# The squares for an RMS norm added up to one tile on VectorE, so that TensorE sums one product in place of two

## The chip, the cores and the metric

One core of one Trainium2 chip. The metric is the device time of one execution of the whole program in microseconds (us), as the median of several runs.

## The reference

The program runs two layers of a hybrid mixer (mLSTM, gated linear attention, sparse attention), and then one block of another kind: a feed-forward part, a mixer (attention and spatial gating), and a second feed-forward part with a final norm. The batch is 1, the sequence 256 tokens, the width 1024, all in float32. In front of each part stands the same norm:

```python
def rmsnorm(x, g):
    xf = x.astype(jnp.float32)
    y = xf * lax.rsqrt(jnp.mean(xf * xf, axis=-1, keepdims=True) + EPS)
    return (y * g.astype(jnp.float32)).astype(x.dtype)

h = h + 0.5 * swiglu(rmsnorm_2(h, ffn1_norm[l]), ffn1_w_gate[l], ffn1_w_up[l], ffn1_w_down[l])
n = rmsnorm_2(h, mix_norm[l])
z = n @ w_in[l]                      # and the mixer on z, which ends with h = h + merged @ w_out[l]
h = h + 0.5 * swiglu(rmsnorm_2(h, ffn2_norm[l]), ffn2_w_gate[l], ffn2_w_up[l], ffn2_w_down[l])
```

What matters here is the mean over the 1024 channels of the squares of each token.

## The kernel before

The residual `x` lies as 8 tiles of 128 channels by 256 tokens. Weights stream in slots of 512 KB (a slot is a 128x1024 tile): SyncE loads a slot into `raw`, ScalarE copies it to the high part in `ring` (L481), and GpSimd (L367, in two pieces of 128x512) or, for some slots, VectorE (L1011, in one piece of 128x1024) subtracts to get the low part. TensorE multiplies high and low parts in three products for each pair of tiles; `slots_used` is its signal that a slot may be filled again.

The norm is not waited for. TensorE starts each part with products on `x` times the gain (`early`, L498, and `early_lo`, L1021), and the factor 1/root(mean) is multiplied into the results afterwards. The parts are numbered: n = 0 and 1 are the two layers, n = 2 the first feed-forward part, n = 3 the mixer, n = 4 the second feed-forward part. For each of them:

- ScalarE squares `x` in four blocks of 128x512 (`squares`, L487); block 0 goes to PSUM, into `ps[3]`.
- VectorE adds the other three to it (`add_squares`, L1028). The first two of these adds stay in PSUM, the third writes its 512 columns to `sqs`, a view of the tile `y`, and releases `sq_sum`. Each add but the last is followed by a wait for its own end (`step`).
- TensorE sums over the partitions: after the first two slots and half of the third (`around_squares`, L1746), it multiplies `ones` with the two halves of `sqs[:, 0:512]`, in `ps[4]` (`sum_squares`, L1726). The wait on `sq_sum` stands in front of the weight load of the first of these products. It then goes on with the other half of the third slot and with the fourth.
- VectorE makes the mean of it (L1004), ScalarE the logarithm and the exponential (L468, L469), VectorE one step of refinement (L1040 to L1044); the factor is then in `rms`. On ScalarE copies of weights (L481) stand between in program order.
- In a feed-forward part VectorE then makes the gate and the up product of tile 0 from the waiting results (L1478, L1483), and L1488, L1492 and L1073 go on with them; TensorE needs the bank of gate 0 for tile 2, after the fourth slot. In the mixer VectorE scales four early results (L1629) and TensorE needs the first of their banks after the fourth slot too.

At n = 4 one more instruction of VectorE stands between its adds and the mean: `split(FFN2_AT - 1)`, the low part of one slot (L1011). At n = 2 and n = 3 none does. The end of the program sums its last squares in another way (L1691, L2350), which the change does not touch.

Of the kernel before, what the change touches and what calls it, by code (L numbers as in the profile page):

```python
# [24 lines left out]
ALU = mybir.AluOpType  # L25
# [5 lines left out]
T = 256  # L31
KT = D // P
LAYERS = 2
# [101 lines left out]
GELU_A, GELU_B = 0.044715, 0.7978845608028654  # L135
N_UPDATES = 4
FINAL = LAYERS + 3
FINAL_AT = (LAYERS + 1) * (KT // 2)


# [14 lines left out]
def build(nc, d, out):  # L155
    ctx = ExitStack()
    with ctx:
# [54 lines left out]
        sqs = y[:, 8:16, :].rearrange("p a t -> p (a t)")  # L212
# [17 lines left out]
        def branch(k, part):  # L230

            return ys[:, k, part, :] if k < 4 else xs[:, k - 4, part, :]
# [18 lines left out]
        ps = [ctx.enter_context(nc.psum_tensor(f"ps{b}", [P, 512], F32)) for b in range(8)]  # L251
# [15 lines left out]
        ones = const[:, C_ONE:C_ONE + P]  # L267
# [23 lines left out]
        def _(sp):  # L291
# [55 lines left out]
            for k in (0, 2, 6, 4):  # L347
                if k == 6:
                    sp.wait_ge(S["last_f"], 1)
                else:  # L350
                    sp.wait_ge(S["x_f"], FINAL_AT + k // 2 + 1)
                sp.dma_start(out[:, k:k + 2, :], xn[:, k:k + 2, :]).then_inc(S["stored"], 16)
# [637 lines left out]
        def _(dve):  # L990
            step = Steps(dve, S["dve_steps"])
            tt, ts, stt = dve.tensor_tensor, dve.tensor_scalar, dve.scalar_tensor_tensor
# [10 lines left out]
            def mean_square(dst, src, n, done):  # L1003
                ts(dst, src, 1.0 / n, EPS, ALU.mult, ALU.add).then_inc(done, 1)  # L1004
# [19 lines left out]
            def add_squares(n):  # L1024

                for b in range(1, 4):
                    dve.wait_ge(S["sq"], n * 4 + b + 1)
                    ins = tt(ps[3][:, :] if b < 3 else sqs[:, 0:512], ps[3][:, :], sqs[:, b * 512:(b + 1) * 512],  # L1028
                             ALU.add)
                    if b < 3:  # L1030
                        step(ins)
                ins.then_inc(S["sq_sum"], 1)

            def factor(n, copy=False):
# [58 lines left out]
            early_lo(0, par, V_G, True, range(4, KT))  # L1093
            split(-RING + 1)
            add_squares(0)
            split(-RING + 3)
            dve.wait_ge(S["const_in"], 16)
            dve.wait_ge(S["par_in"], 16)

            for it in range(LAYERS):  # L1100
# [367 lines left out]
                update_x(it, it * LAYER_SLOTS + LAYER_SLOTS, 1.0)  # L1468
                early_lo(it + 1, par, V_G)
                add_squares(it + 1)  # L1470
                split(LAYER_SLOTS - 1, it, LAYER_SLOTS)


            def ffn(at, n, h_done, y_done, last):
# [55 lines left out]
                if not last:  # L1530
                    update_x(n, at + FFN_SLOTS, 0.25)
                    early_lo(n + 1, par2, U_MIX)
                    add_squares(n + 1)
                    for p in range(at + FFN_SLOTS - 2, at + FFN_SLOTS):
                        split(p)
# [145 lines left out]
            def end_update(a, b):  # L1681

                dve.wait_ge(S["end_out"], a // 2 + 1)
                dst = flat(x[:, a:b, :])
                stt(dst, ps[4 + a // 2][:, a % 2 * T:a % 2 * T + (b - a) * T], 0.25, dst, ALU.mult, ALU.add)\
                    .then_inc(S["end_x"], 1)
# [14 lines left out]
            end_update(7, 8)  # L1701
            dve.wait_ge(S["ssq"], FINAL + 1)
            mean_square(var[:, 0:2], ps[4][:, 0:2], D, S["end_var"])
# [12 lines left out]
        def _(pe):  # L1716
            mm = pe.matmul

            def sum_squares(n):

                if n == 0:
                    pe.wait_ge(S["bias_sb"], 1)
                    pe.wait_ge(S["const_in"], 16)
                pe.wait_ge(S["sq_sum"], n + 1)
                for c in range(2):
                    last = mm(ps[4][:, 0:T], ones, sqs[:, c * T:(c + 1) * T], start=(c == 0), stop=(c == 1))  # L1726
                last.then_inc(S["ssq"], 1)

            PARTS = ((0, 0), (1, 0), (0, 1))
# [1 line left out]
            def tile_product(bank, half, slot, rhs, ks=range(KT), at=0, ready=None, freed=False, first=True, final=True):  # L1731

                order = [(k, w, x) for k in ks for w, x in PARTS]
                if ready:
                    order = [(k, w, 0) for k in ks for w in (0, 1)] + [(k, 0, 1) for k in ks]
                for i, (k, wp, xp) in enumerate(order):
                    if ready and wp == 0:
                        ready(k, xp)
                    last = mm(ps[bank][:, half * T:(half + 1) * T],  # L1739
                              ring[:, slot % RING, wp, (at + k) * P:(at + k + 1) * P], rhs(k, xp),  # L1740
                              start=(first and i == 0), stop=(final and i == len(order) - 1))
                    if freed and (wp, xp) == PARTS[-1] and k < KT - 1:
                        last.then_inc(S["xs_free"], 1)
                return last

            def around_squares(bank, slot, n):  # L1746

                tile_product(bank, 0, slot, xs_part, range(KT // 2), final=False)
                sum_squares(n)
                tile_product(bank, 0, slot, xs_part, range(KT // 2, KT), first=False).then_inc(S["slots_used"], 1)  # L1750
# [571 lines left out]
            for n in range(KT):  # L2322
# [7 lines left out]
                for g in range(2):  # L2330
                    last = tile_product(n % 4, g, slot, lambda k, part: branch(4 * g + k, part), range(4), at=4 * g,
                                        ready=(lambda k, part: pe.wait_ge(
                                            S["b_lo" if part else "b_hi"], 4 * g + k + 1)) if n == 0 else None)
# [28 lines left out]
            for b in (5, 6):  # L2362
                for c in range(2):
                    last = pe.transpose(ps[b][:, c * P:(c + 1) * P], rms[:, 512 + c:513 + c].broadcast_to((P, P)), ident)
# [129 lines left out]
```

## Time and profile before

| | |
|---|---|
| median of 3 runs | 1122.24 us (1121.80 to 1122.39) |
| profiled execution | 1122.59 us |
| its span, first to last instruction | 1120.8 us |
| TensorE busy | 1111.9 us (99%) |
| VectorE, ScalarE, GpSimd busy | 722.6, 664.2, 731.6 us |

The page gives sums for each engine, the chain of work that ended last, and the costliest groups of instructions. The timeline gives instructions in order of time: start in us from the begin of the span, duration in us, engine, line, operation, tiles and count. PE is TensorE's multiplication, PEld its weight load, DVE VectorE, ACT ScalarE and POOL GpSimd. A matmul's end is modelled and its records overlap, so the start of the weight loads (PEld) is the better clock for TensorE. A row with a count above 1 merges neighbours of the same kind, and its duration reaches from the first start to the last end. The text in brackets is idle time of the engine just before the instruction, and what ended it.

### The profile page before, as it was taken

To read this page: it belongs to the slowest core of one execution; us is meant where nothing else is said; L and a number is where in the kernel's file an instruction comes from. 1 tells how busy PE (TensorE), PEld (TensorE's weight loads), DVE (VectorE), ACT (ScalarE), POOL (GpSimd) and SP (SyncE) were. 2 spreads that over 40 slices of the span, in tenths; PEclk is the share of its full clock that TensorE was granted. 3 is DMA by queue.
4 is the path that set the end of the run, shared out by engine and by line. 5 is a ranking of instruction groups with operands and counts; after the bars stand their busy time and mean duration, and the time that the engine had idled before them with its cause. 6 is when DMAs were issued, how large, how long until landed. Compare 5 with 4: busy or idle time off the path is not lost.

```text
span 1120.8 us, 22358 instructions
## 1 busy us (share of the span) xinstructions
PE 1111.9 (99%) x8968; PEld 1063.0 (95%) x8968; DVE 722.6 (64%) x1275; ACT 664.2 (59%) x1098; POOL 731.6 (65%) x575
## 2 busy tenths in 40 slices
PE   9999999999999999999999999999999999999997
PEld 7888999999988899899999999999899999999997
DVE  5886655577589675375848655556769567655554
ACT  7676754575567577356647544446566547544444
POOL 6787697668488868865865655445865774544442
PEclk9999999999999999999999999999999999999999
DMA  9563354556555534545566766664644655666651
GB/s 335 172 194 119 129 177 150 177 161 216 159 170 188 161 127 151 176 152 170 189 209 207 223 198 193 195 196 144 215 149 134 206 190 169 220 194 190 189 188 38
DMA packets 63895, 199.49 MB, mean 178 GB/s; under 512 B 6992, under 2 KB 17968, under 8 KB 63792
## 3 DMA queue, kind: packets, MB, share of 16 engines
q1 hardware_dynamic: 61920, 194.99, 53.9%
q10 hardware_dynamic: 1872, 3.08, 0.8%
q8 instruction: 71, 1.16, 0.4%
q14 instruction: 32, 0.26, 0.1%
HBM read 196.21 MB, written 1.84 MB: 177 GB/s over the span
## 4 chain that ended last, share of the span: by engine, by line
PE 96%; ACT 2%; DMA 1%; DVE 0%; issue 0%; POOLq 0%; SPq 0%; ACTq 0%
PE ps L1739 51%; PE ps L1837 19%; PE ps L1815 14%; PE ps L1996 2%; PE ps L1788 1%; PE ps L2173 1%; ACT ring L481 1%; PE ps L2093 1%; DMA x<-in_x 1%; PE ps L2070 1%; PE ps L2031 1%; ACT xs L498 0%; PE ps L1970 0%; PE ps L2057 0%; PE ps L2073 0%; PE ps L2094 0%
## 5 line engine op out<-in xcount | busy, mean ns | idle before, releaser
L367 POOL TENSOR_TENSOR ring<-raw,ring 128x512 fp32r<-128x512 f32 x514 | 699.0, 1366 | 364.2 <-ACT ring L481 343.2
L1739 PE MATMUL ps<-xs,ring 128*128 128x256 f32 x5040 | 597.7, 278 | 0.4 <-DVE mq L1049 0.3
L1739 PEld LDWEIGHTS ps<-xs,ring 128*128 128x128 f32 x5040 | 582.9, 188 | 3.6 <-issue 1.3
L481 ACT ACTIVATE ring<-raw 128x1024 fp32r<-128x1024 f32 x364 | 383.2, 1057 | 215.3 <-PE ps L1739 119.3
L1837 PE MATMUL ps<-ys,ring 128*128 128x256 f32 x1920 | 224.4, 276 | 0.0
L1837 PEld LDWEIGHTS ps<-ys,ring 128*128 128x128 f32 x1920 | 220.7, 188 | 0.0
L1011 DVE TENSOR_TENSOR ring<-raw,ring 128x1024 fp32r<-128x1024 f32 x107 | 144.9, 1355 | 69.3 <-ACT ring L481 68.9
L1815 PE MATMUL ps<-ring,xs 128*128 128x512 f32 x672 | 164.9, 397 | 0.0
L1815 PEld LDWEIGHTS ps<-ring,xs 128*128 128x128 f32 x672 | 123.6, 188 | 26.8 <-issue 1.3
L1329 DVE SCALAR_TENSOR_TENSOR ca<-ps,par,ca 128x253 f32<-128x253 f32 (+2 forms) x96 | 46.0, 479 | 34.4 <-ACT ca L564 33.0
L1483 DVE SCALAR_TENSOR_TENSOR ca<-ps,rms 128x256 f32<-128x256 f32 x44 | 18.6, 423 | 48.7 <-PE ps L1739 48.7
L1478 DVE SCALAR_TENSOR_TENSOR ex<-ps,rms 128x256 f32<-128x256 f32 x44 | 18.6, 423 | 45.1 <-PE ps L1739 44.9
L1073 DVE TENSOR_TENSOR ys<-y,ys 128x256 fp32r<-128x256 f32 x32 | 30.9, 969 | 16.6 <-ACT ys L730 16.6
L820 ACT ACTIVATE ys<-ca 128x256 fp32r<-128x256 f32 x44 | 18.4, 418 | 34.8 <-DVE ca L1492 34.8
L1073 DVE TENSOR_TENSOR ys<-ca,ys 128x256 fp32r<-128x256 f32 x44 | 30.4, 691 | 11.0 <-ACT ys L820 11.0
L1488 DVE TENSOR_TENSOR ca<-ca,ex 128x256 f32<-128x256 f32 x44 | 30.8, 700 | 1.5
L581 ACT ACTIVATE ex<-ps 128x256 f32<-128x256 f32 x32 | 12.2, 382 | 30.7 <-PE ps L1739 30.7
L564 ACT ACTIVATE ca<-ps,par 128x256 f32<-128x256 f32 x32 | 17.9, 560 | 21.0 <-PE ps L1739 21.0
L498 ACT ACTIVATE xs<-x,par 128x256 fp32r<-128x256 f32 x40 | 16.7, 497 | 13.1 <-DVE x L1083 9.6
L1492 DVE SCALAR_TENSOR_TENSOR ca<-ex,ca 128x256 f32<-128x256 f32 x44 | 22.2, 506 | 1.4
L1788 PE MATMUL ps<-xs,ring 128*128 128x256 f32 x192 | 22.4, 276 | 0.0
L1788 PEld LDWEIGHTS ps<-xs,ring 128*128 128x128 f32 x192 | 22.1, 188 | 0.0
(291 smaller groups left out, 1027.2 us busy)
## 6 DMA issues: line engine op xcount, KB each, us to landing
raw<-in_w SPq DMA_DIRECT2D x364, 512.0 KB, 3.6
y<-bias_rows SPq DMA_DIRECT2D x6, 256.0 KB, 4.3
out_y<-y SPq DMA_DIRECT2D x4, 256.0 KB, 2.4
const<-in_const SPq DMA_DIRECT2D x1, 896.0 KB, 12.3
bias_rows<-lg ACTq DMA_DIRECT2D x1, 768.0 KB, 8.4
x<-in_x ACTq DMA_DIRECT2D x1, 512.0 KB, 4.5
x<-in_x SPq DMA_DIRECT2D x1, 512.0 KB, 6.9
dec<-in_wT ACTq DMA_DIRECT2D x1, 512.0 KB, 3.7
```

Source lines behind the costliest of these rows:

```text
L367: last = pool.tensor_tensor(ring[:, g % RING, 1, part], raw[:, g % RAW, part], ring[:, g % RING, 0, part].bitcast(F32), ALU.subtract)
L481: act.activation(ring[:, g % RING, 0, :], raw[:, g % RAW, :], ACT.Copy).then_inc(S["hi"], 1)
L1011: tt(ring[:, g % RING, 1, :], raw[:, g % RAW, :], ring[:, g % RING, 0, :].bitcast(F32), ALU.subtract).then_inc(lo[g % RAW], 1)
L1073: tt(ys[:, at, 1, :], src, ys[:, at, 0, :].bitcast(F32), ALU.subtract).then_inc(S["y_lo"], 1)
L1329: ins = stt(dst[:, late:T], bank[:, 0:T - late], w[:, j:j + 1], dst[:, late:T], ALU.mult, ALU.add)
L1488: step(tt(ca[:, f % 2, :], ca[:, f % 2, :], ex[:, 2 + f % 2, :], ALU.mult))
L1492: stt(ca[:, f % 2, :], ex[:, f % 2, :], 1.0, ca[:, f % 2, :], ALU.add, ALU.mult)\
L1739: last = mm(ps[bank][:, half * T:(half + 1) * T], ring[:, slot % RING, wp, (at + k) * P:(at + k + 1) * P], rhs(k, xp), start=(first and i ...
L1788: return mm(ps[bank][:, 0:T], ring[:, slot % RING, wp, k * P:(k + 1) * P], rhs(k, xp), start=start, stop=stop)
L1815: last = mm(ps[banks[tt]][:, :].rearrange("p (j c) -> p j c", j=4), xs[:, 2 * q + k, xp, tt * P:(tt + 1) * P], w, start=(q == 0 and k == 0 ...
L1837: ins = mm(ps[4 + n // 2][:, n % 2 * T:(n % 2 + 1) * T], ring[:, slot % RING, wp, n * P:(n + 1) * P], ys[:, at, xp, :], start=(first and n ...
L1996: last = mm(second(ps[6 + e][:, (2 * tt + pr) * P:(2 * tt + pr + 1) * P]), kk[rows, keys], second(qq[rows, queries]), start=True, stop=True)
```

## The change

For n from 2 on (`FOLDED = LAYERS`, so the two feed-forward parts and the mixer) VectorE waits for the end of its third add and makes a fourth: it adds the second 256 columns of `sqs` to the first 256. `sq_sum` is released by this fourth add. TensorE then multiplies `ones` with `sqs[:, 0:256]` only. Layers 0 and 1 stay as they are.

```diff
+FOLDED = LAYERS
@@ add_squares(n), VectorE
                     ins = tt(ps[3][:, :] if b < 3 else sqs[:, 0:512], ps[3][:, :], sqs[:, b * 512:(b + 1) * 512],
                              ALU.add)
-                    if b < 3:
+                    if b < 3 or n >= FOLDED:
                         step(ins)
+                if n >= FOLDED:
+                    ins = tt(sqs[:, 0:T], sqs[:, 0:T], sqs[:, T:2 * T], ALU.add)
                 ins.then_inc(S["sq_sum"], 1)
@@ sum_squares(n), TensorE
                 pe.wait_ge(S["sq_sum"], n + 1)
-                for c in range(2):
-                    last = mm(ps[4][:, 0:T], ones, sqs[:, c * T:(c + 1) * T], start=(c == 0), stop=(c == 1))
+                parts = 1 if n >= FOLDED else 2
+                for c in range(parts):
+                    last = mm(ps[4][:, 0:T], ones, sqs[:, c * T:(c + 1) * T], start=(c == 0), stop=(c == parts - 1))
                 last.then_inc(S["ssq"], 1)
```

## Rows read from the trace of the kernel before

**Rows 1.** The page: busy time of the engines, and the chain that ended last.
```profile
PE 1111.9 (99%) x8968; PEld 1063.0 (95%) x8968; DVE 722.6 (64%) x1275; ACT 664.2 (59%) x1098; POOL 731.6 (65%) x575
...
PE 96%; ACT 2%; DMA 1%; DVE 0%; issue 0%; POOLq 0%; SPq 0%; ACTq 0%
```

**Rows 2.** One line's instructions, L1726: duration (min/median/max ns), and who waited for it.
```profile
L1726 PE MATMUL ps<-y,const x20: 377/378/379, 16.8 to 938.3; 128*128 128x256 f32 x20
...
  DVE ps L1004: 6.5, 5
```

**Rows 3.** Timeline around the sum of squares of n = 2, from narrow windows.
```profile
595.32 1.44 DVE L1028 TENSOR_TENSOR ps<-ps,y 128x512 f32<-128x512 f32 x2
596.53 1.30 POOL L367 TENSOR_TENSOR ring<-raw,ring 128x512 fp32r<-128x512 f32 x1 [9.47 <-ACT ring L481]
596.79 0.69 DVE L1028 TENSOR_TENSOR y<-ps,y 128x512 f32<-128x512 f32 x1
597.91 0.30 PEld L1726 LDWEIGHTS ps<-y,const 128*128 128x128 f32 x2
597.91 1.28 POOL L367 TENSOR_TENSOR ring<-raw,ring 128x512 fp32r<-128x512 f32 x1
598.67 0.19 PEld L1739 LDWEIGHTS ps<-xs,ring 128*128 128x128 f32 x1
...
601.92 0.42 DVE L1478 SCALAR_TENSOR_TENSOR ex<-ps,rms 128x256 f32<-128x256 f32 x1
```

**Rows 4.** Page and timeline: VectorE on two SBUF inputs, GpSimd beside it.
```profile
L1488 DVE TENSOR_TENSOR ca<-ca,ex 128x256 f32<-128x256 f32 x44 | 30.8, 700 | 1.5
...
601.77 1.30 POOL L367 TENSOR_TENSOR ring<-raw,ring 128x512 fp32r<-128x512 f32 x1
602.71 0.63 DVE L1488 TENSOR_TENSOR ca<-ca,ex 128x256 f32<-128x256 f32 x1
...
641.05 1.30 POOL L367 TENSOR_TENSOR ring<-raw,ring 128x512 fp32r<-128x512 f32 x1
641.72 0.91 DVE L1488 TENSOR_TENSOR ca<-ca,ex 128x256 f32<-128x256 f32 x1
...
1110.05 0.42 DVE L1691 TENSOR_TENSOR y<-y 128x256 f32<-128x256 f32 x1
```

**Rows 5.** Timeline around the sum of squares of n = 3.
```profile
776.99 1.30 POOL L367 TENSOR_TENSOR ring<-raw,ring 128x512 fp32r<-128x512 f32 x1 [6.79 <-ACT ring L481]
777.19 0.69 DVE L1028 TENSOR_TENSOR y<-ps,y 128x512 f32<-128x512 f32 x1
778.31 0.73 PEld L1726 LDWEIGHTS ps<-y,const 128*128 128x128 f32 x4
779.18 1.06 ACT L481 ACTIVATE ring<-raw 128x1024 fp32r<-128x1024 f32 x1
779.48 0.43 DVE L1004 TENSOR_SCALAR ps<-ps 128x256 f32<-128x256 f32 x1 [1.60 <-PE ps L1726]
780.14 0.36 ACT L468 ACTIVATE rms<-ps 128x256 f32<-128x256 f32 x1
```

**Rows 6.** Timeline: TensorE's first wait after the factor of n = 3.
```profile
783.14 0.43 DVE L1629 SCALAR_TENSOR_TENSOR mq<-ps,rms 64x256 f32<-64x256 f32 x1
783.62 0.19 PEld L1739 LDWEIGHTS ps<-xs,ring 128*128 128x128 f32 x1 [0.28 <-DVE mq L1629]
```

**Rows 7.** Timeline around the sum of squares of n = 4.
```profile
936.60 0.69 DVE L1028 TENSOR_TENSOR y<-ps,y 128x512 f32<-128x512 f32 x1
937.21 1.22 DVE L1011 TENSOR_TENSOR ring<-raw,ring 128x1024 fp32r<-128x1024 f32 x1
937.57 0.73 PEld L1726 LDWEIGHTS ps<-y,const 128*128 128x128 f32 x4
938.56 1.29 POOL L367 TENSOR_TENSOR ring<-raw,ring 128x512 fp32r<-128x512 f32 x1 [6.38 <-ACT ring L481]
938.74 0.43 DVE L1004 TENSOR_SCALAR ps<-ps 128x256 f32<-128x256 f32 x1 [0.32 <-PE ps L1726]
```

## The prediction

> **What bounds the kernel now.** I read the page first. TensorE is busy in 99% of the span, and the chain that ended last is TensorE for 96% [rows 1]. So a piece of TensorE work that goes is worth its full length, unless the place where it stood was covered by a wait; and a wait that is put in front of TensorE costs its full length. VectorE, ScalarE and GpSimd are busy in about two thirds and matter only where TensorE stands waiting for them. Next I read the one line that the change shortens: the product of `ones` with the squares appears 20 times, four records in each of five places, and the only engine that waits for it is VectorE [rows 2]. The change touches three of the five places: the first feed-forward part (n = 2), the mixer (n = 3) and the second feed-forward part (n = 4). For each I then read the timeline, to see when the last add of VectorE ends, when TensorE comes to the wait on `sq_sum`, and what GpSimd does meanwhile [rows 3, 5, 7].
>
> **What goes.** Each float32 product is two records. At n = 2 the four weight loads of the two products start at 597.91 and 598.02 (the second row covers both) and the next line's load at 598.67: after the first, the loads are (598.67 - 598.02) / 3 = 0.215 us apart [rows 3]. One product less takes two of these steps away: **0.43 us** at each of the three places, 1.29 us in all if nothing else moved. The products that are left and the sum that they accumulate cost the same.
>
> **What comes.** VectorE gets a fourth add, 128x256, which must wait for the third to be through. The adds of 0.70 start 0.735 apart (595.32 to 596.79 for two), so such a dependent step costs 0.035 us between [rows 3]. TensorE's wait for `sq_sum` now stands behind that add. Before the change the third add ended at 596.79 + 0.69 = 597.48 and TensorE came to the wait at 597.91, thus 0.43 us of cover; the new step and add use that up and more. Behind TensorE's waiting load stand the second half of the tile product and everything after it, so an overrun is paid in full.
>
> The trace of before has no add of two 128x256 tiles of squares at this place, so I bound it. VectorE's operation of that size with both inputs in SBUF takes 0.42 us when GpSimd stands still, and 0.63 or 0.91 when it starts inside a piece of GpSimd's subtraction: then it ends 0.28 us after that piece ends (601.77 + 1.30 = 603.07 against 602.71 + 0.63 = 603.34; 641.05 + 1.30 = 642.35 against 641.72 + 0.91 = 642.63) [rows 4]. The line of the first two, 44 operations with a mean of 0.70, shows how common being held up is [rows 4]. The third add of squares, with one input in PSUM, keeps its 0.69 beside a running piece of GpSimd [rows 3]. So the place decides the price. The Trainium skill (SBUF — State Buffer, "Who interferes with whom") speaks against this change in just this way: a VectorE instruction with two SBUF inputs is held up whole by a GpSimd instruction that reads SBUF and started earlier, one with a PSUM input is not. By that rule, the trace agrees; a sum that priced the new add at its free 0.42 everywhere would give the second rival below.
>
> **n = 2.** The new add can start at 597.52. GpSimd's piece runs from 596.53 to 597.83 [rows 3], so the add ends at 598.11. From the end of a VectorE operation to the load that waits for it are 0.05 us (783.14 + 0.43 = 783.57, load at 783.62 [rows 6]). TensorE's load comes at 598.16, 0.26 later than before; less 0.43 that is **-0.17 us**. Does the next wait eat it? The product after the two early slots needs the gate of tile 0, which VectorE ends at 601.92 + 0.42 = 602.34 [rows 3]; TensorE needs it 36 loads after 598.67, at about 602.8, so some 0.3 us of room stay. The factor does not come earlier with the shorter sum, since ScalarE has a copy of weights ahead of it, as at n = 3 below.
>
> **n = 3.** The new add can start at 777.92, GpSimd's piece ends at 776.99 + 1.30 = 778.29, the add at 778.57, and TensorE's load goes from 778.31 to 778.62 [rows 5]. 0.31 lost and 0.43 won would be -0.12. But here TensorE stands 0.28 us idle soon after, at 783.62, for VectorE's early results [rows 6], and these hang on the factor. The factor's chain does not start with the squares: VectorE's mean ends at 779.48 + 0.43 = 779.91, and ScalarE takes it only at 780.14, because its copy of 779.18 + 1.06 stands in front of it [rows 5]. The sum 0.12 earlier moves nothing in this chain; TensorE comes earlier to its wait and stands longer. **0.** The cover in the other direction is 780.14 - 779.96 = 0.18 us: only a sum that is later than before by more than this would move the mixer.
>
> **n = 4.** GpSimd is in no piece before 938.56, so the add takes 0.42: from 936.60 + 0.69 + 0.035 = 937.33 to 937.75, TensorE's load at 937.80 against 937.57 before [rows 4, 7]. 0.23 lost, 0.43 won: **-0.20 us**. VectorE's weight split of 937.21 is queued behind the add and goes 0.46 later, to end at about 938.89; the mean behind it started at 938.74 and now starts some 0.1 later. The gate of tile 0 has 0.4 us of room or more there (same order as at n = 2), so this costs nothing; the slot that the split makes ready is used only at about 942.5.
>
> **GpSimd**, held up by the new add, gets later by up to 0.28 us at n = 2 and 3. The slot that it makes ready first at n = 2 is complete at 597.91 + 1.28 = 599.19 and used 12 loads after 598.67, at about 600.1 [rows 3], so nothing of it shows. Nothing moves in the DMA queues but by these tenths.
>
> **Sum:** -0.17 + 0 - 0.20 = -0.37 us. The profiled execution took 1122.59 us (span 1120.8 and 1.79 around it), 0.35 over the median of 1122.24; the profile should thus show 1122.2 and the median **1121.9 us**. That is 0.03%. A measurement of this kernel tells about 0.2% (2.24 us) from no change.
>
> **The rivals.**
> (a) *The add is never held up*: 0.42 at each place. n = 2 is then at 597.52 + 0.42 + 0.05 = 597.99, -0.35; n = 3 stays at 0, n = 4 at -0.20: 1121.7. Against it stand the held operations of rows 4.
> (b) *Everything is won*: -1.29, 1120.9. It would need that TensorE came later to its wait than I read, and that the idle time in the mixer did not take its share. Rows 3, 5 and 6 speak against it.
> (c) *The wait eats the gain*: starting again after a wait costs TensorE 0.2 us more at each place than the move of its load, for instance because the load cannot be hidden under a running product. Then 0 in sum, 1122.2. For it: the load after the idle time of rows 6 has no product to run under. Against it: the loads behind that one follow at their usual distance.
> (d) *Slower: GpSimd keeps the access to SBUF between its pieces.* The pieces at n = 2 follow 0.08 us apart (597.83, next at 597.91 [rows 3]). If VectorE, which has waited since 597.52, does not get in between, the add ends with the next piece, 597.91 + 1.28 + 0.28 = 599.47, and TensorE's load at 599.52: +1.61 - 0.43 = +1.18. The same in the mixer gives -0.12 + 1.36 = +1.24, of which the cover of 0.18 hides a part, +1.06. With n = 4 unchanged +2.04: 1124.3. If it loses a second piece at both places, another 1.25 to 1.3 each, +4.6: 1126.8, slower by 0.4%. It decides from two pieces on. Against it: in rows 4 VectorE gets in each time after the piece in which it began to wait.
>
> **How the numbers follow.** Forecast 0.71, (a) 0.10, (b) 0.03, (c) 0.08; (d) with one piece lost 0.03 and with two 0.04. Faster by over 0.2% is none of these, since even the whole of the work removed is 1.29 us; I leave 0.01 for what I overlook. Slower is the last case, 0.04; the same 0.95. Range: the runs of before scatter 0.3 us about their median, and so may those of after; from (a) less 0.6 that is 1121.1 as the lower end. The upper end takes in (c), and a piece lost at n = 2 alone (+1.18 - 0.20, 1123.2).
>
> **What would show it.** Per place two records of the sum of squares in place of four. A fourth VectorE operation of about 0.60 us at n = 2, 0.66 at n = 3, 0.42 at n = 4, ending 0.28 after GpSimd's piece in the first two. TensorE's load waiting 0.2 to 0.3 us each time, on VectorE. The idle time in the mixer at L1629's results grown from 0.28 to about 0.4. Wrong would be: an add over 0.7 us, a new idle time of TensorE anywhere later, or a mean-to-root step of ScalarE that starts other than just behind its copy.

## The result and the profile after

The kernel with the change takes **1128.62 us** in the median of 22 runs, against 1122.32 for the kernel before: a ratio of 1.0053 (95% interval 1.0037 to 1.0070). It is slower by 0.5%, outside my range of 1121.1 to 1123.2, and on the side to which I gave 0.04.

The median hides what happened. The 22 times of the change lie in three groups with nothing between: 7 from 1121.70 to 1122.49, 9 from 1128.25 to 1129.30, and 6 from 1135.19 to 1135.70. The kernel before has one group, 1121.80 to 1123.27. A second series of 12 runs (e1 below) gave 6, 5 and 1 in the same three groups. So the change is as fast as I said in some executions, and 6.9 or 13.5 us slower than that in the others. Two single executions of later experiments, 1392.73 us in e4 and 1235.88 in e8, had a mean granted TensorE clock of 0.751 and 0.85 where all others had 0.997 or 0.998, and are left out of their groups.

The profiled execution of the change fell in the short group (1121.9 us, span 1120.1). There nearly every step of the prediction can be read. Timeline around the sum of squares of n = 2, 3 and 4, kernel after, from narrow windows (L1029 is the third add, L1034 the new one, L1730 the load for the product of the squares, L1743 the load for the products around it, which is L1739 in the kernel before):

```profile
595.86 1.31 POOL L368 TENSOR_TENSOR ring<-raw,ring 128x512 fp32r<-128x512 f32 x1 [9.48 <-ACT ring L482]
596.11 0.69 DVE L1029 TENSOR_TENSOR y<-ps,y 128x512 f32<-128x512 f32 x1
596.83 0.62 DVE L1034 TENSOR_TENSOR y<-y 128x256 f32<-128x256 f32 x1
597.51 0.19 PEld L1730 LDWEIGHTS ps<-y,const 128*128 128x128 f32 x1 [0.20 <-DVE y L1034]
597.83 0.19 PEld L1743 LDWEIGHTS ps<-xs,ring 128*128 128x128 f32 x1
...
776.17 1.30 POOL L368 TENSOR_TENSOR ring<-raw,ring 128x512 fp32r<-128x512 f32 x1 [6.80 <-ACT ring L482]
776.35 0.69 DVE L1029 TENSOR_TENSOR y<-ps,y 128x512 f32<-128x512 f32 x1
777.08 0.67 DVE L1034 TENSOR_TENSOR y<-y 128x256 f32<-128x256 f32 x1
777.80 0.19 PEld L1730 LDWEIGHTS ps<-y,const 128*128 128x128 f32 x1 [0.25 <-DVE y L1034]
782.82 0.19 PEld L1743 LDWEIGHTS ps<-xs,ring 128*128 128x128 f32 x1 [0.41 <-DVE mq L1632]
...
935.80 0.69 DVE L1029 TENSOR_TENSOR y<-ps,y 128x512 f32<-128x512 f32 x1
936.52 0.42 DVE L1034 TENSOR_TENSOR y<-y 128x256 f32<-128x256 f32 x1
937.00 0.19 PEld L1730 LDWEIGHTS ps<-y,const 128*128 128x128 f32 x1 [0.16 <-DVE y L1034]
937.32 0.19 PEld L1743 LDWEIGHTS ps<-xs,ring 128*128 128x128 f32 x1
```

Measured from the start of the third add, so that the two executions compare. At n = 2 the load of the squares comes 1.40 us after it (597.51 - 596.11), before the change 1.12 [rows 3]: 0.28 later, forecast 0.26. The load behind the squares comes 1.72 after it in place of 1.88, so 0.16 are won, forecast 0.17. At n = 3 the load that waits for VectorE's results comes 6.47 after the third add (782.82 - 776.35), before 6.43 [rows 5, 6]: nothing won, forecast 0. At n = 4 the load of the squares comes 1.20 after in place of 0.97 [rows 7], 0.23 later as forecast, which leaves 0.20 won. The new add takes 0.62, 0.67 and 0.42 us, forecast 0.60, 0.66 and 0.42; at n = 2 it ends at 597.45, 0.28 after GpSimd's piece (597.17). The sum of these is -0.32 us, forecast -0.37.

Where the other groups come from needs the profile of a long execution.

### The profile page after: what moved, and what is told of

It reads as the page before. It is cut to its first block, busy times and chain, and to the rows that moved or that the text cites. A ratio compares the mean times of both kernels' runs of the same rounds, so it can differ in the third digit from the quotient of the medians.

```text
span 1120.1 us, 22349 instructions
## 1 busy us (share of the span) xinstructions
PE 1111.1 (99%) x8962; PEld 1062.2 (95%) x8962; DVE 726.2 (65%) x1278; ACT 665.3 (59%) x1098; POOL 732.4 (65%) x575
## 4 chain that ended last, share of the span: by engine, by line
PE 96%; ACT 2%; DMA 1%; DVE 0%; issue 0%; POOLq 0%; SPq 0%; ACTq 0%
PE ps L1743 51%; PE ps L1841 19%; PE ps L1819 14%; PE ps L2000 2%; PE ps L1792 1%; PE ps L2177 1%; ACT ring L482 1%; PE ps L2097 1%; PE ps L2074 1%; DMA x<-in_x 1%; PE ps L2035 1%; ACT xs L499 0%; PE ps L1974 0%; PE ps L2061 0%; PE ps L2077 0%; PE ps L2098 0%
## 5 line engine op out<-in xcount | busy, mean ns | idle before, releaser
L1743 PE MATMUL ps<-xs,ring 128*128 128x256 f32 x5040 | 597.5, 278 | 0.6 <-DVE mq L1052 0.4
L1743 PEld LDWEIGHTS ps<-xs,ring 128*128 128x128 f32 x5040 | 582.8, 188 | 3.8 <-issue 1.3
L1396 DVE SCALAR_TENSOR_TENSOR ps<-ex,ps 128x256 f32<-128x256 f32 x32 | 13.6, 424 | 13.2 <-ACT ex L582 13.2
```

Of the source, the lines that this page charges most:

```text
L1743: last = mm(ps[bank][:, half * T:(half + 1) * T], ring[:, slot % RING, wp, (at + k) * P:(at + k + 1) * P], rhs(k, xp), start=(first and i ...
```

## The experiments

**e1: the change again.**

> The changed kernel as it is, to see the spread of its times again and, with luck, a profile of a long execution. Its 22 executions lie in three groups, near 1121.9 (7), 1128.7 (8) and 1135.3 us (7), where the kernel before has one, 1121.8 to 1123.3. Theory A: an event of 6.7 us happens at two of the three changed places, each in about half of the executions, independently; then the same three groups come, about 1 : 2 : 1. If the profile is of a long execution, one stretch of 6.7 us must show TensorE idle or slowed right behind a sum of squares. Rival B: the two longer groups belong to the chip or the session and not to the kernel; then one group at 1121.9.

Measured: 12 runs, 6 from 1121.60 to 1122.23, 5 from 1128.82 to 1129.41, 1 at 1135.91. The three groups come again, as theory A says. Rival B falls: the kernel before ran again beside the experiments, 78 executions in four sessions, all from 1121.80 to 1123.18. The profiled execution was of the middle group (1129.13, span 1127.3). Its waits are those of the short one, and no new gap is in it. The difference is in the count of products in a stretch of fixed length. Busy time by stretch (busy us of PE and number of its instructions, then PEld, DVE, ACT, POOL; granted clock; DMA share; GB/s), first for the kernel before, then for e1:

```profile
620.00:770.00 150.00, 150.00 (x1326) 150.00 (x1325) 80.84 (x119) 71.86 (x92) 77.64 (x63) 1.00 0.64 200
950.00:1100.00 150.00, 150.00 (x1326) 150.00 (x1325) 84.72 (x124) 72.93 (x94) 75.54 (x57) 1.00 0.59 187
```

```profile
620.00:770.00 150.00, 150.00 (x1276) 150.00 (x1275) 77.82 (x115) 69.39 (x90) 72.35 (x59) 1.00 0.58 192
950.00:1100.00 150.00, 150.00 (x1326) 150.00 (x1325) 87.37 (x126) 74.12 (x97) 75.05 (x56) 1.00 0.59 196
```

In 150 us of the first feed-forward part e1 gets 1276 products done, the kernel before 1326. TensorE is busy all the time in both and the granted clock is 1.00 of the upper level in both. So a load and product pair of 256 columns takes 150 / 1326 = 0.1131 us in one and 150 / 1276 = 0.1176 in the other, 4% more, one after the other, from the sum of squares of n = 2 to that of n = 3. In the second feed-forward part this execution of e1 ran at the short pace. The chain that ended last shows the same, 48 products in each piece (start, us, what), kernel before and e1:

```profile
611.30 5.44 PE ps L1739 x48
619.46 5.44 PE ps L1739 x48
```

```profile
611.29 5.65 PE ps L1743 x48
619.77 5.65 PE ps L1743 x48
```

The distances of the starts, read one by one, are 113 or 114 ns at the short pace and 116 to 120 at the long one (means 113.3 and 117.8). From 598.5 to 784.7 e1 has 1582 products in a row at the long pace: 1582 x 4.45 ns = 7.0 us. The first two groups of the change are 6.9 us apart.

**e2, e3, e4: one place at a time.** Edit, with 2, 3 or 4:

```diff
-FOLDED = LAYERS
+FOLDED = (2,)
-                    if b < 3 or n >= FOLDED:
+                    if b < 3 or n in FOLDED:
-                if n >= FOLDED:
+                if n in FOLDED:
-                parts = 1 if n >= FOLDED else 2
+                parts = 1 if n in FOLDED else 2
```

> The fourth add and the shorter sum at n = 2 alone; n = 3 and 4 as before. My forecast without any event: 0.37 - 0.20 less gain, about 1122.1. Theory A1 (the event needs an add that GpSimd holds up, as at n = 2 and n = 3): two groups, 1122.1 and 1128.8, each about half. Theory A2 (the event needs TensorE to come to its wait before the release, at any of the three places): two groups too. Rival C (the event is at n = 3 or 4 alone, or needs all changes together): one group at 1122.1.

> The same at n = 3 alone. Without any event: 1122.2, no change from before. A1 and A2: two groups, 1122.2 and 1128.9. Rival C with the event at n = 2 or 4: one group.

> The same at n = 4 alone, where the add is not held up by GpSimd. Without any event: 1122.0. A1: one group at 1122.0. A2: two groups, 1122.0 and 1128.7; since three such places would give up to three events, and the changed kernel shows no group near 1142, A2 needs that the event is rarer here.

Measured. e2: two groups, 6 runs from 1121.75 to 1122.69 and 6 from 1128.52 to 1129.50. e3: one group, 11 runs from 1121.81 to 1122.77. e4: 8 runs from 1121.80 to 1122.43 and 3 from 1129.31 to 1129.67. So the events belong to n = 2 and n = 4, one each, and A1 falls: GpSimd's hold on the add is not what they need, since n = 4 has none, and n = 3 has it and no long runs. The profiled execution of e4 was a long one, with the long pace in the second part alone:

```profile
620.00:770.00 150.00, 150.00 (x1326) 150.00 (x1325) 81.08 (x119) 71.67 (x92) 77.70 (x63) 1.00 0.61 200
950.00:1100.00 150.00, 150.00 (x1276) 150.00 (x1275) 81.09 (x119) 70.30 (x91) 72.62 (x55) 1.00 0.56 187
```

A2 stands for these two places; at n = 3 its forecast of two groups missed. Why n = 3 costs nothing follows from the length of the row: only some 36 pairs lie between its squares and the next wait, so the long pace there can cost 0.16 us, inside a wait. Behind the squares of a feed-forward part follow more than 1500 pairs of one shape with nothing between them. This also speaks against a change of the alignment of TensorE's program as the cause: e2 takes two records out at n = 2 and keeps n = 4 short, e3 takes two out at n = 3 and keeps n = 4 short.

**e5: the wait without the shorter sum.** Edit to the change:

```diff
-                    ins = tt(sqs[:, 0:T], sqs[:, 0:T], sqs[:, T:2 * T], ALU.add)
+                    ins = tt(ps[3][:, 0:T], sqs[:, 0:T], sqs[:, T:2 * T], ALU.add)
-                parts = 1 if n >= FOLDED else 2
+                parts = 2
```

> The fourth add as in the change, at n = 2, 3 and 4, but into a spare half of a PSUM bank, and TensorE still sums both products of the squares, after waiting for that add: the wait without the shorter sum. Theory P (after TensorE has stood at a wait, its load and product pairs run at one of two paces, 113.3 or 117.8 ns for 256 columns, by chance, until another kind of work breaks the row): three groups as with the change itself, only each 0.43 us later at n = 2 and n = 4, near 1122.8, 1129.5 and 1136. The profile shows rows of some 1580 products at n = 2 or 1523 at n = 4 at 117 to 119 ns if it is of a long execution. Rival Q (one float32 product in place of two is what leaves the pace to chance): one group at 1122.8.

Measured: 3 runs from 1122.81 to 1123.32, 8 from 1129.72 to 1130.41, 1 at 1136.65. Theory P holds, the places of the groups too: with both products kept, the wait alone makes the pace a matter of chance. The profiled execution was of the middle group. Both parts have the wait (0.19 us at n = 2, 0.17 at n = 4) and the same four records; the first part ran at the short pace, the second at the long one:

```profile
620.00:770.00 150.00, 150.00 (x1326) 150.00 (x1325) 81.07 (x119) 71.36 (x91) 77.39 (x63) 1.00 0.64 200
950.00:1100.00 150.00, 150.00 (x1276) 150.00 (x1275) 81.21 (x119) 70.01 (x92) 72.43 (x54) 1.00 0.61 188
```

Waits that none of these edits put in show the same. In the mixer TensorE waits for VectorE's early results in the kernel before and in e4, which leaves the mixer as it was. The wait is 0.28 us in both, and the products in front of it are the same. The 96 loads behind it take 10.97 us in one profile and 11.37 in the other, 4.2 ns more for each step:

```profile
783.62 10.97 PEld L1739 LDWEIGHTS ps<-xs,ring 128*128 128x128 f32 x96 [0.28 <-DVE mq L1629]
783.41 11.37 PEld L1743 LDWEIGHTS ps<-xs,ring 128*128 128x128 f32 x96 [0.28 <-DVE mq L1632]
```

**e6, e7: the shorter sum without the wait.** Edit to the change, for n from 2 on, +1 in e6 and +2 in e7:

```diff
-                tile_product(bank, 0, slot, xs_part, range(KT // 2), final=False)
+                at = KT // 2 + (1 if n >= FOLDED else 0)
+                tile_product(bank, 0, slot, xs_part, range(at), final=False)
                 sum_squares(n)
-                tile_product(bank, 0, slot, xs_part, range(KT // 2, KT), first=False).then_inc(S["slots_used"], 1)
+                tile_product(bank, 0, slot, xs_part, range(at, KT), first=False).then_inc(S["slots_used"], 1)
```

> The change, but the sum of squares stands behind 5 of the 8 channel tiles of the third slot in place of 4: three products or 0.34 us later, so that TensorE comes to the wait just after the fourth add is through (0.31 us at most). Theory P: no wait at n = 2 and 4, so no choice of pace: one group at 1122.3 - 0.43 - 0.43 = 1121.5. Rival Q: three groups, 1121.5, 1128.2 and 1135.

> As before, but behind 6 of the 8 tiles: 0.68 us later, with 0.4 us of room. Theory P: one group at 1121.5, or up to 0.3 later if the mixer's factor, whose sum now comes 0.25 us later than before, passes its cover of 0.18. Rival Q: three groups. Should e6 still show a few long executions and this one none, the room in e6 was too small.

Measured: e6 four runs from 1134.93 to 1135.14, e7 four from 1134.90 to 1135.47. Both theories missed the time. No wait of TensorE at the squares is left in their traces, and there is one group only, as P said; but it is the longest one. Both feed-forward parts ran at the long pace, e6:

```profile
620.00:770.00 150.00, 150.00 (x1276) 150.00 (x1275) 78.13 (x116) 69.64 (x90) 72.29 (x59) 1.00 0.62 193
950.00:1100.00 150.00, 150.00 (x1276) 150.00 (x1275) 83.33 (x122) 70.97 (x93) 72.87 (x55) 1.00 0.62 192
```

So without a wait the pace of the two feed-forward parts is fixed, not free: short in each of the runs of the kernel before, where there are two, long in each of these, where there is one.

**e12: the control for e6.** The kernel before with the same move by three products, both products kept, no fold.

> The kernel before with both products of the squares, moved behind 5 of the 8 channel tiles of the third slot, as in e6, without the fourth add. The control for e6: if moving the sum alone made it long, this is near 1136; if the missing second product did, as theory R says, one group at 1122.3 to 1122.6.

Measured: 10 runs from 1122.16 to 1122.90, ratio 1.0001 (0.9992 to 1.0011), both parts at the short pace:

```profile
620.00:770.00 150.00, 150.00 (x1326) 150.00 (x1325) 81.41 (x120) 71.33 (x92) 77.50 (x63) 1.00 0.64 200
950.00:1100.00 150.00, 150.00 (x1326) 150.00 (x1326) 84.72 (x124) 73.06 (x94) 75.91 (x58) 1.00 0.60 187
```

The move is innocent; the missing second product makes e6 long. (The fourth add that e6 also has stands in e5 too, and there the pace was short in some executions.)

**e8: a wait far from any float32 product.** Edit to the kernel before:

```diff
-                        pe.wait_ge(S["y_lo"], y_done + f - 1)
+                        pe.wait_ge(S["y_lo"], y_done + (f if last and f == 12 else f - 1))
```

> The kernel before with nothing of the change, but in the second feed-forward part, at tile 12 of 22, TensorE waits for one low part of a product earlier than it needs it, about 0.65 us in front of a load of weights, with no float32 product near. Theory P: two groups. The short one at 1122.3 + 0.65 = 1123.0; the long one more by the products left, about 765 x 4.45 ns = 3.4 us, at 1126.4. Rival Q, or that the squares are needed for it: one group at 1123.0.

Measured: 8 runs from 1122.53 to 1123.29, 2 at 1126.42 and 1126.52. The step is 3.6 us, expected 3.4: half of a part, half of the price. The profiled execution was a short one, so the long pace was not seen here, only its time, and in two executions. The wait, its only new one, is small:

```profile
1023.99 0.30 PEld L1739 LDWEIGHTS ps<-xs,ring 128*128 128x128 f32 x2 [0.34 <-DVE ys L1073]
```

**e9, e10, e11, e13, e14, e15: what fixes the pace where no wait stands.** e9, e10 and e13 change e6, the others the kernel before. The core of each, in this order:

```diff
+                    mm(ps[4][:, T:T + 1], ones, ones[:, 0:1], start=True, stop=True)         # e9, ahead of the product
+                    last = mm(ps[4][:, T:T + 1], ones, ones[:, 0:1], start=True, stop=True)  # e10, behind it
+                    last = mm(ps[4][:, T:2 * T], ones, sqs[:, 0:T], start=True, stop=True)   # e11, a third one
+                        last = mm(ps[4][:, c * P:(c + 1) * P], ones, sqs[:, c * P:(c + 1) * P], start=True, stop=True)  # e13, c = 0, 1
+                    last = mm(ps[4][:, :], ones, sqs[:, 0:2 * T], start=True, stop=True)     # e14, in place of the two
+                    last = mm(ps[4][:, T:2 * T], ones, sqs[:, c * T:(c + 1) * T], start=True, stop=True)  # e15, c = 0, 1, behind the two
```

> The kernel of e6 (one product of the squares, no wait, always long at 1135.0) with one more float32 product of one column, of constants into a spare column of PSUM, just ahead of the product of the squares; it should cost about 0.22 us at each place. Theory R (after the float32 products the pairs settle at one pace or the other by how many such products, or records, came directly before; two gave the short pace, one the long): two products again, so one group at 1121.5 + 2 x 0.22 = 1121.9. Rival S (what counts is the time between the last fp32r pair and the next, 0.43 us longer with two full products): the small product is not enough, one group near 1135.4.

> The same, the one-column product behind the product of the squares. Theory R: 1121.9. Rival S: near 1135.4. A third outcome, short here and long in e9 or the other way round, would say that the last float32 product alone sets the pace.

> The kernel before with a third full float32 product (a repeat of the first, into a spare half of a bank) at n = 2, 3 and 4, no new wait. Its own cost is 0.43 us at n = 2 and 4 and about 0.25 at n = 3: 1123.4 at the short pace. Theory R in the form that one product of any kind flips the pace: odd numbers are long, 1123.4 + 7.0 + 6.8 = 1137.2. In the form that two or more settle it: 1123.4.

> The kernel of e6 (fold, sum three products later, no wait, always long), with its one product of 256 columns cut in two of 128: four records as in the kernel before, in about the time of one full product. If the number of records picks the pace, short: 1121.5. If the time of the float32 work does, long as e6: 1135.0.

> The kernel before with the two products of the squares as one of 512 columns at n = 2, 3 and 4: two records, as in e6, in the time of two full products. The squares of half of the channels are then left out of the means, so the factors are larger; nothing else is. If the number of records picks the pace, long: 1122.3 + 13.8 = 1136. If the time does, short: 1122.3.

> The kernel before with two more full float32 products (repeats into a spare half bank): four. Own cost 0.86 us at n = 2 and 4 and about 0.7 at n = 3: 1124.7 at the short pace. If even numbers of full products are short, one group there; if only two is, long at 1138.5.

In e14 the squares of half of the channels are missing from the means, so it computes something else; only its time is of use.

Measured, four runs each, all in one group at the time that the long pace gives. The profiles of e6, e7 and of these six all show 1276 products in both stretches of 150 us.

| | float32 products at each place | us | pace at n = 2 and 4 |
|---|---|---|---|
| before, e12 | 256 + 256 columns | 1121.80 to 1123.27; 1122.16 to 1122.90 | short |
| e6, e7 | 256 | 1134.93 to 1135.14; 1134.90 to 1135.47 | long |
| e9 | 1 + 256 | 1135.66 to 1136.39 | long |
| e10 | 256 + 1 | 1135.46 to 1136.10 | long |
| e13 | 128 + 128 | 1134.79 to 1135.11 | long |
| e14 | 512 | 1135.49 to 1135.94 | long |
| e11 | three of 256 | 1137.25 to 1137.54 | long |
| e15 | four of 256 | 1138.50 to 1138.70 | long |

The number of records does not decide (four of them are short in the kernel before, long in e9, e10 and e13), nor the time of the float32 work (0.86 us is short as two products and long as one wide one), nor parity (four are long). At n = 2 and n = 4 the pairs in front of the squares run at the short pace in all of these kernels, and of eight arrangements only the one that the kernel before has is followed by the short pace there.

The kind of the products is not all, though. At n = 3 the same arrangements stand behind the long row of the first part, again without a wait, and some of them change the pace back. The loads between the last float32 product and the next wait, in e13, e10, e9 and e6:

```profile
785.23 3.83 PEld L1746 LDWEIGHTS ps<-xs,ring 128*128 128x128 f32 x33
785.50 3.95 PEld L1745 LDWEIGHTS ps<-xs,ring 128*128 128x128 f32 x33
785.71 3.93 PEld L1745 LDWEIGHTS ps<-xs,ring 128*128 128x128 f32 x33
785.22 4.06 PEld L1743 LDWEIGHTS ps<-xs,ring 128*128 128x128 f32 x33
```

The first two rows compare with each other, and so do the last two, since their first step is of one length (0.11 us in e13 and e10, 0.22 in e9 and e6). e13 and e9 went from the long pace to the short one, e10 and e6 stayed long. Read load by load, the profiles give this, one profile for most entries:

| float32 products, no wait | behind the short pace | behind the long pace |
|---|---|---|
| 256 + 256 | short | short (e2 at n = 3) |
| 256; 256 + 1; 512 | long | long |
| 1 + 256; 128 + 128; three of 256; four of 256 | long | short |

So the pace behind the products hangs on their kind and on the pace in front of them together. At n = 3 this is worth 0.16 us at most and can't be seen in the times. Which property of the products does this stays open. e13, meant to beat both kernels, is 1.1% slower than before, and no version here beats the kernel before.

## Why the prediction was wrong

The bookkeeping of the change held, step by step: 0.43 us for each product that goes, the held add, the move of TensorE's load, nothing won in the mixer, 0.3 us in all. In about 4 executions out of 10 (13 of 34) that is the whole story. (The prediction's sentence on the add at 0.42 everywhere points to "the second rival"; it is the first, (a).)

The step that failed is in the sentence that a wait in front of TensorE "costs its full length", and in my handling of rival (c). I asked there whether starting again costs TensorE something beyond the move of its load, put it at 0.2 us for each place, gave it 0.08, and argued it away because "the loads behind that one follow at their usual distance". I took this distance for a constant of TensorE. It is one of two, 113.3 and 117.8 ns for a pair of 256 columns, and what stands before the row of pairs bears on which. The missing term was 1582 x 4.45 = 7.0 us at n = 2 and 1523 x 4.45 = 6.8 us at n = 4, each in about 4 executions of 10, where I had 0.2. This is from the mix of the groups: of the 34 runs of the change 13 have no long part, 14 one and 7 both, thus 28 of 68 parts; e2 alone has 6 of 12.

The same step failed a second time in the gain. There a piece of TensorE work that goes "is worth its full length", 0.43 us at each place, and changes nothing behind it. With the wait out of the way (e6) the shorter sum should have given 1121.5 us and gave 1135.0.

Two effects of the change act together. The shorter sum by itself made both parts long in every run (e6, e7: eight runs near 1135). The new wait by itself makes each part long in some runs (e5). With both the pace is left to chance too, so the change, at 1128.62 in the median, is spared part of what its own shorter sum would cost at 1135.

Rival (d), my slower case, did not happen: in the profiled executions of the change the add got in after the piece in which it began to wait. The side was right for a wrong reason, which is no help. The 1.29 us of "the whole of the work removed" bounds the gain only. For the loss I had no bound, and my chances for it covered rival (d) alone.

Could the profile before have told it? In part. It shows no long row right behind a sum of squares, but it shows both paces. The chain that ended last, in the mixer of the kernel before (start, us, what):

```profile
824.13 0.33 PE ps L2248 x3
824.46 0.22 PE ps L2239 x2
824.68 0.43 PE ps L2240 x2
825.12 2.83 PE ps L1739 x24
827.94 0.43 PE ps L2259 x2
828.37 0.22 PE ps L2260 x2
828.59 2.74 PE ps L1739 x24
```

The same 24 products take 2.83 us behind L2240 and 2.74 behind L2260, four times in turn. A difference of 0.09 us in a row of 24 is 4 ns a product, and I passed over it as noise. Multiplied by the length of the row that follows the edit it is the largest number in this case.

The profile before also has a long row behind a wait of TensorE, in the first layer. e12 runs the same instructions up to n = 2 and shows the short pace there. First the kernel before, then e12:

```profile
22.24 5.71 PEld L1739 LDWEIGHTS ps<-xs,ring 128*128 128x128 f32 x48 [0.53 <-DVE mq L1049]
21.87 5.51 PEld L1739 LDWEIGHTS ps<-xs,ring 128*128 128x128 f32 x48 [0.55 <-DVE mq L1049]
```

Against rival (c) I had read only the wait in the mixer, behind which this profile happens to be short.

The Trainium skill's rule on the port that VectorE shares with GpSimd (SBUF — State Buffer, "Who interferes with whom") held at all three places: the new add was held at n = 2 and n = 3 (0.62 and 0.67 us) and free at n = 4 (0.42 us). Its price is small beside the pace.

## What to carry to other kernels

Where TensorE bounds a kernel with a long unbroken row of equal products, what stands just before the row deserves more care than its own cost: a float32 product taken away or a wait of 0.2 us put in can change the pace of everything behind it. Look for the two paces in the profile before (the same number of products with two durations), and price a wait or a break as its length plus the row behind it times the difference. And time such an edit in ten or more executions: the one profiled execution of the change fell in the short group, and a few runs can do so too.

## What the runs showed of the hardware

- TensorE runs rows of fp32r load and product pairs (128x128 weights, 256 columns) at one of two lasting paces, 113.3 or 117.8 ns a pair, at the same granted clock of 1.00 (1326 and 1276 products in 150 us). A row keeps its pace through changes of line and of weights, here for 1582 products, up to the next float32 product or wait.
- Behind a wait of TensorE of 0.17 to 0.34 us the pace varied from one execution of the same program to the next: with both float32 products kept 9 of 12 runs have a long part (e5), with no such product near 2 of 10 have the longer time (e8). The two paces also stand behind one and the same wait of 0.28 us in two profiles (10.97 and 11.37 us for 96 loads).
- Without a wait, and with pairs at the short pace in front, the pace behind float32 products was the same in every run: long behind seven kinds of them, short behind exactly two of 256 columns. With the long pace in front four of the seven kinds were followed by the short pace, in one profile each.
- VectorE's add of two SBUF tiles of 128x256 ended 0.28 us after the GpSimd piece in which it started (0.62 and 0.67 us), and took 0.42 with GpSimd idle.
